# First modulation in two halves with the queries by feature tiles, and RWKV's first pair prepared among the products of k and v

## The reference, cut to what matters

```
def adaln_in(s, cvec, norm_g, mod_w, mod_b):
    m = jax.nn.silu(cvec) @ mod_w + mod_b
    shift, scale, gate = jnp.split(m, 3, axis=-1)
    return rmsnorm(s, norm_g) * (1.0 + scale) + shift, gate
...
    hx, gate_x = adaln_in(x, c_lat, norm_g, mod_w, mod_b)
    hc, gate_c = adaln_in(ctx, c_cx, norm_g, mod_w, mod_b)
    px = hx @ w_in
    pc = hc @ w_in
```

```
    r, k, v = products of lerp(0), lerp(2), lerp(3) with three 1024 x 1024 matrices
    w_log = -softplus(-(w0[d] + tanh(lerp(1) @ w1[d]) @ w2[d])) - 0.5 ;  decay = exp(-exp(w_log))
    a = sigmoid(a0[d] + (lerp(4) @ a1[d]) @ a2[d]) ;  k_d = k * (1.0 + (a - 1.0) * k_a)
    g = sigmoid(lerp(5) @ g1) @ g2 ;  kk = normalised k * k_k
```

## Time and profile before

| | |
|---|---|
| median of 3 runs | 4120.06 us (4116.69 to 4125.03) |
| the profiled execution's own time | 4123.75 us |
| its span in the profile | 4122.5 us (1.25 us lie outside) |
| TensorE busy | 90% of the span, 31840 instructions |
| VectorE, ACT, POOL busy | 40%, 29%, 33% |
| mean granted clock of TensorE | 0.936 |
| data moved | 263.76 MB, mean 64 GB/s |

### The profile page before, as it was taken

How to read it: one execution, slowest core, us unless ns; L and a number is a source line. 1 busy time by engine, 2 the same in 40 slices (tenths; PEclk the granted TensorE clock), 3 DMA queues, 4 the chain that set the end, 5 groups by cost and what they waited for, 6 DMA issues and landing times.

```text
span 4122.5 us, 72507 instructions
## 1 busy us (share of the span) xinstructions
PE 3700.5 (90%) x31840; PEld 2364.9 (57%) x31840; DVE 1657.6 (40%) x2926; ACT 1191.1 (29%) x2160; POOL 1377.5 (33%) x1214
## 2 busy tenths in 40 slices
PE   7998778999898988889899999898788888889998
PEld 3755565434444455555455555354566666748887
DVE  1344343223444122444433233532655555533334
ACT  3253222221212174432300000201555565520001
POOL 1320442011212112656432323351543343425444
PEclk9998687988999999989999999999899999989999
DMA  5420000521101211540111111222000000022222
GB/s 194 146 94 21 2 1 11 205 84 33 33 23 51 82 46 64 178 158 21 51 56 57 62 61 52 97 81 77 3 16 15 28 15 15 14 82 82 92 82 72
DMA packets 196131, 263.76 MB, mean 64 GB/s; under 512 B 6087, under 2 KB 151495, under 8 KB 193640
## 3 DMA queue, kind: packets, MB, share of 16 engines
q1 hardware_dynamic: 188880, 242.78, 17.6%
q10 hardware_dynamic: 6936, 16.35, 1.0%
HBM read 246.52 MB, written 12.58 MB: 63 GB/s over the span
## 4 chain that ended last, share of the span: by engine, by line
PE 72%; ACT 8%; DVE 6%; issue 6%; POOL 5%; DMA 2%; SPq 0%; ACTq 0%; DVEq 0%; POOLq 0%
PE ps L236 57%; PE ps L2943 2%; PE ps L759 2%; PE ps L484 1%; ACT mem L836 1%; PE ps L1959 1%; PE ps L786 1%; POOL mem L2846 1%; PE ps L774 1%; PE ps L378 1%; DMA mem<-rkv 1%; DVE mem L1159 1%; PE ps L493 1%; PE ps L1277 1%; DVE mem L817 1%
## 5 line engine op out<-in xcount | busy, mean ns | idle before, releaser
L236 PE MATMUL ps<-mem 64*64 64x64 f32 (+6 forms) x25344 | 2744.1, 304 | 203.2 <-ACT mem L661 35.9
L236 PEld LDWEIGHTS ps<-mem 64*64 64x64 f32 (+1 forms) x25344 | 1779.6, 156 | 1179.5 <-issue 606.0
L2846 POOL TENSOR_TENSOR mem<-mem 128x256 f32<-128x256 f32 (+1 forms) x264 | 238.5, 920 | 356.7 <-ACT mem L3301 185.3
L854 POOL TENSOR_SCALAR mem<-mem 128x768 f32<-128x768 f32 (+2 forms) x128 | 219.2, 1725 | 199.4 <-DVE mem L820 199.3
L2141 ACT ACTIVATE mem<-ps 128x384 f32<-128x384 f32 (+1 forms) x80 | 35.7, 446 | 838.8 <-PE ps L236 788.3
L2128 POOL TENSOR_TENSOR mem<-mem 128x512 f32<-128x512 f32 (+1 forms) x80 | 100.1, 1251 | 440.9 <-PE ps L236 392.2
L2152 DVE TENSOR_TENSOR mem<-mem,ps 128x384 f32<-128x384 f32 (+1 forms) x80 | 39.9, 499 | 442.9 <-PE ps L236 442.9
L2943 PE MATMUL ps<-mem 128*128 128x128 f32 x960 | 180.5, 307 | 32.3 <-DVE mem L2868 21.4
L591 POOL TENSOR_TENSOR mem<-mem 128x512 f32<-128x512 f32 (+1 forms) x72 | 74.7, 1062 | 393.3 <-ACT mem L586 391.6
L2876 ACT ACTIVATE mem<-ps 128x256 f32<-128x256 f32 (+1 forms) x220 | 101.5, 461 | 198.7 <-PE ps L2943 198.5
L2868 DVE TENSOR_TENSOR mem<-mem,ps 128x256 f32<-128x256 f32 (+1 forms) x220 | 109.5, 513 | 116.7 <-PE ps L236 116.1
(11 more groups left out here) (326 smaller groups left out, 4049.1 us busy)
## 6 DMA issues: line engine op xcount, KB each, us to landing
mem<-i_mod_w SPq DMA_DIRECT2D x48, 1024.0 KB, 6.8
mem<-i_ffn_wg SPq DMA_DIRECT2D x22, 1024.0 KB, 5.1
mem<-i_ffn_wu SPq DMA_DIRECT2D x22, 1024.0 KB, 5.2
mem<-i_e_w_in SPq DMA_DIRECT2D x16, 1024.0 KB, 6.0
mem<-i_o_w_in SPq DMA_DIRECT2D x16, 1024.0 KB, 5.6
mem<-i_ffn_wd SPq DMA_DIRECT2D x16, 1024.0 KB, 5.3
mem<-i_e_mod_w SPq DMA_DIRECT2D x12, 1024.0 KB, 6.0
mem<-i_o_mod_w SPq DMA_DIRECT2D x12, 1024.0 KB, 7.3
```

The source lines that it names most:

```text
L236: ins = e.h.matmul(out, l, r, start=(i == 0), stop=(i == n - 1))
L854: K.pool.h.tensor_scalar(w, w, stat(i, o, 1), None, MUL).then_inc(*nm.up(tag, i, o))
L2846: K.pool.h.tensor_tensor(m3(self.slot(l)), self.lraw, bm(C(K, f"cm{self.d}", l, 64), 2 * self.np), MUL).then_inc(*self.mk.up(key, l))
```

## The change

Two places are changed. At the start of the program:

- SP loads only the first 266 columns of the constants (`ident`, `ones`, `eps`, `sel`) at first; the others and ctx are loaded behind the second half of the modulation.
- The four jobs of the modulation become two halves: half 0 gives shift and scale of feature tiles 0 to 3 (jobs 0 and 8 of `e_mod_b`), half 1 those of tiles 4 to 7. They have a ring of four slots of their own. SP's order is half 0 (four slabs), two slabs of `e_w_in`, half 1 (four slabs), ctx, the other constants.
- x is normalised and modulated for tiles 0 to 3 after half 0, for tiles 4 to 7 after half 1 (`factors(j)` makes the scales of a half).
- The queries are done with `across=2`: four output tiles in four banks, feature tile by feature tile, and `beside` puts TensorE's steps of half 1 after feature tiles 1, 2 and 3, and the sums of ctx's squares after tile 5. ctx has a norm of its own (`nc`, "ec").

In RWKV:

- `jobs` is r, w, a, g, k, v.
- `Scan` is made before `rwkv_inputs`, with the first pair's tiles laid where `u` and `xx` lie (free once the last mixture is made). `Scan.ahead` advances front(0) on every engine by counted steps at the middle and end of the units of k and v (`AHEAD`), with banks from those that were just used (`FIRST`). `load_first` loads pair 0's r, k and head weights behind k's first unit, and its v behind v's first unit. v of pair 0 is turned in the middle of the last unit (`values_pe`, `values_act`).
- Before the scan only VectorE, ACT and POOL wait for the others' ends (`fence(but=K.pe)`); `run` begins with work(0).

The core of the diff:

```
+    mod = modulate(K, A, B)
+    ring = Ring(K, "mslab", [K.alloc(SLOT) for _ in range(4)], "e")
+    halves = [mod_stream(K, (4, 5), 6, mod_jobs(("e_mod_b", 4 * j, 4 * j + 4), ("e_mod_b", 8 + 4 * j, 12 + 4 * j)), ring) for j in range(2)]
...
+    def sp():
+        run(halves[0][2]())
+        linear_sp(K, I["e_w_in"], (0, 512))
+        run(halves[1][2]())
+        K.sp.h.dma_start(K.xc, I["ctx"]).then_inc(*lc.up(0, by=16))
+        K.sp.h.dma_start(K.cn[:, CN_FIRST:], I["consts"][:, CN_FIRST:]).then_inc(*lr.up(by=16))
...
+    def dve():
+        steps = halves[0][1]()
+        next(steps)
+        q = n.factors(K.dve, 0)
+        for j in range(2):
+            for k in range(4 * j, 4 * j + 4):
+                K.dve.h.tensor_tensor(tile(k), K.xt[:, k, :], q, MUL).then_inc(*ml.up("e", 0, k))
+            if j == 0:
+                for _ in steps:
+                    pass
+                factors(0)
+        run(halves[1][1]())
+        factors(1)
+
+    def act():
+        for j in range(2):
+            K.act.wait_ge(*sc.at("e", j, 1))
+            for k in range(4 * j, 4 * j + 4):
+                K.act.wait_ge(*ml.at("e", 0, k))
+                mod(k, 0, tile(k)).then_inc(*out.up("e", 0, k))
+
+    def beside():
+        steps = halves[1][0]()
+        yield
+        for _ in range(3):
+            next(steps)
+            yield
+        yield
+        nc.sums()
+        yield
     n.squares()
-    for _ in range(3):
-        next(steps)
+    steps = halves[0][0]()
+    next(steps)
     n.sums()
     run(steps)
...
+    nc.squares()
+    linear_pe(K, "nq", (0, 512), hap, RNG[:1], ALL, K.sig("qk_copy", "act"), beside(), across=2)
...
-    jobs = [("rr", 0, W[0], 1024, RNG[:1], 0), ("rk", 2, W[1], 1024, RNG, 512), ("rv", 3, W[2], 1024, RNG, 1280),
-            ("rw", 1, I["w1"], 128, RNG, (hw, ACT.Tanh)), ("ra", 4, I["a1"], 128, RNG, (ha, ACT.Copy)), ("rg", 5, I["g1"], 128, RNG[:1], (hg, ACT.Sigmoid))]
+    jobs = [("rr", 0, W[0], 1024, RNG[:1], 0), ("rw", 1, I["w1"], 128, RNG, (hw, ACT.Tanh)), ("ra", 4, I["a1"], 128, RNG, (ha, ACT.Copy)),
+            ("rg", 5, I["g1"], 128, RNG[:1], (hg, ACT.Sigmoid)), ("rk", 2, W[1], 1024, RNG, 512), ("rv", 3, W[2], 1024, RNG, 1280)]
...
-                for i, p in order:
+                for q, (i, p) in enumerate(order):
                     if p == 1:
                         units[n][i].take()
                     units[n][i].product(p)
+                    if i and p == (3 if i == 1 else 2):
+                        scan.ahead("pe", 4 * (n - 4) + i, "mid", [(q - j) % 8 for j in range(1, 5)])
...
+AHEAD = {(1, "mid"): 3, (2, "mid"): 8, (3, "mid"): 13, (5, "mid"): 16, (5, "end"): 19, (6, "mid"): 22, (6, "end"): 25}
+FIRST = {2: "ss", 3: "a", 5: "w0", 6: "w1", 7: "v"}
...
+    def ahead(self, e, unit, part, banks=None):
+        if banks and unit in FIRST:
+            self.first[FIRST[unit]] = banks
+        while self.steps[e] < AHEAD.get((unit, part), 0):
+            next(self.early[e], None)
+            self.steps[e] += 1
+        if (unit, part) == (7, "mid") and e in ("pe", "act"):
+            (self.values_pe if e == "pe" else self.values_act)(0)
...
+    def load_first(self, v):
+        K, b, s = self.K, self.bufs[0], self.ld[0]
+        if v:
+            K.sp.wait_ge(*s.at(0, "k"))
+            K.sp.h.dma_start(b[:, 1664:2432], K.rkv[0][:, 1280:2048]).then_inc(*s.up(0, by=16))
+            return
+        K.sp.h.dma_start(b[:, 0:384], K.ins["hpw"][0]).then_inc(*s.up(0, 0, by=16))
+        K.sp.h.dma_start(b[:, 384:1664], K.rkv[0][:, 0:1280]).then_inc(*s.up(0, "k", by=16))
...
-            run(f(0))
```

More of the change, by code:

```diff
@@ L383, in linear_pe @@
                         K.spent(held[j // 2][0], lin, tag, j)
+            if beside:
+                next(beside, None)
         i = 2 * across
@@ new lines, in even @@
+    sc, ml, out = K.sig("scales", "dve"), K.sig("nrm_mul", "dve"), K.sig("nrm_out", "act")
+    sq, acc, rs = [mem[:, 0:768], mem[:, 768:1536]], mem[:, 1536:2304], mem[:, 2304:3072]
+    n = Norm(K, "e", xt_ap(K), RNG[:1], lambda ri, k: (lx, (0,)), sq, acc, rs, (7,))
+    nc = Norm(K, "ec", xt_ap(K), RNG[1:], lambda ri, k: (lc, (0,)), sq, acc, rs, (7,))
+    halves = [mod_stream(K, (4, 5), 6, mod_jobs(("e_mod_b", 4 * j, 4 * j + 4), ("e_mod_b", 8 + 4 * j, 12 + 4 * j)), ring) for j in range(2)]
+    tile = lambda k: ht[:, k, 0:NX]
@@ L1023, in deltanet @@
 def deltanet(K, ht, hap, ot):
-    I, W = K.ins, K.ins["e_w_in"]
+    for e in (K.pe, K.dve, K.act, K.pool):
+        e.wait_ge(*K.sig("ld_rest").at())
     qT, kT = K.a3(4, NX), K.a3(4, NT)
@@ L2597, in rwkv @@
     mark1 = K.top
[L2598 to L2601, removed]
+    scan = Scan(K, hw, ha, hg, id64)
+    top, K.top = K.top, mark1
+    rwkv_inputs(K, hw, ha, hg, norm, scan)
+    K.fence(but=K.pe)
+    K.top = top
+    scan.run()
     yo_done = K.sig("fi_out", "dve")
@@ L2604, in rwkv @@
     yo = K.yo
-    K.ring.lend([(yo_done, (6,))], [(yo_done, (7,))], [(yo_done, (7,))])
+    K.ring.lend([(scan.wp, (7, d, 1, "wkv")) for d in range(2)], [(yo_done, (7,))], [(yo_done, (7,))])
     def ready(k, r0, rn):
@@ L2663, in operand @@
         return half(n, 2 * j, 1) if p == 7 else {5: t1, 6: t2, 4: t4}[p][:, j, :]
-    units = {n: [Seven(K, jobs[n][0], i, 4, 384, mem, lambda p, j, n=n: operand(n, p, j), wide[i % 2], b) for i, b in enumerate(seven_banks(order, 4))] for n in (1, 2)}
+    units = {n: [Seven(K, jobs[n][0], i, 4, 384, mem, lambda p, j, n=n: operand(n, p, j), wide[i % 2], b) for i, b in enumerate(banks)] for n in (4, 5)}
     def over(n):
@@ L2706, in dve @@
                 lerp(n, k)
-            if n - 1 in units:
-                results(n - 1)
+        for n in units:
+            results(n)
     def results(n):
@@ L2789, in sp @@
     def sp(t):
-        for tag, j, w, cols, rngs, _ in jobs:
+        for n, (tag, j, w, cols, rngs, _) in enumerate(jobs):
             linear_sp(K, w, (0, cols))
+            if n in units:
+                for x in range(2):
+                    K.sp.wait_ge(*st[x].at(8 + 16 * (n - 4) + x))
+                if n == 4:
+                    K.sp.wait_ge(*lp.at(3, KT - 1))
+                scan.load_first(n == 5)
         for i in range(t - 4, t):
@@ L3010, in loads @@
         K.settle(K.sp)
-        for hp in range(8):
+        for hp in range(1, 8):
             if hp >= 2:
@@ L3081, in front_act @@
             yield
[L3082 to L3087 removed]
+        if hp:
+            self.values_act(hp)
         A.wait_ge(*fd.at(hp, "max", 1))
```

165 lines of the change are left out of this document (100 added, 65 removed).

## The result

The changed kernel takes 4074.32 us (median of 4 runs, 4072.09 to 4082.58) beside 4121.92 for the kernel before (4 runs in turn with them, 4116.69 to 4125.03). The ratio is 0.9888, with a 95% interval of 0.9875 to 0.9901: faster by 1.1%, 47.6 us of medians. Forecast were 4077, in 4064 to 4092.

The account below looks back on a forecast made before the run. TensorE was taken as the bound (72% of the chain ending last), paying where it idles or runs at lower clock. RWKV −42 and start −3 gave −45: 4079 from the profiled execution, 4075 from the median, so 4077, range 4064 to 4092.

Parts of the forecast that it names:

- 1, v's last product to the inverse: RWKV, front(0) off the path: 49.8 us become 6.0 (4.5 to 8), gain 43.8 (41.8 to 45.3).
- 2, the front's work on TensorE in the units: RWKV, front(0)'s TensorE work among the unit products is not hidden: cost 7 us (5 to 13).
- 3, waits on the other engines: RWKV units: the front's steps on other engines are ready before TensorE asks, 0 us (bound 12); rival of stalls 0.12.
- 4, v's start: RWKV, v's first nine unit products run with next to no idle time, 23.3 us for 31.4: gain 8.1 (6 to 8.1).
- 5, k's start: RWKV, k's mixture and POOL's turns slow each other, 2.3 us idle: cost 2.5 us (0 to 6).
- the start: Start of the program: queries end at 72.1 us against 75.1, gain 3 (−7 to +1); rival of no gain 0.12.
- The thirteenth turn: k's start: POOL's last turn needed by product 5, there at 22.6 us, wanted at 24.0, so in time.
- The limit: RWKV units: TensorE comes to a bank held by VectorE's wait at `kk0` only past 38 us of k.
- The strict form of the rule: k's start: each turn waits for one mixture, thirteenth turn at 26.1 us, step 5 costing 4.4 instead of 2.5.
- the wait before tile 4: Start: TensorE waits some 1.9 us for bias, scales and ACT; a clock drop costing 1.7 only in the bound.
- the slow first products: Start: the query products' half-clock beginning costs 3 us, as before the change.
- ctx's sums: Start: 0.9 us on TensorE, plus 1 for ACT, which can square ctx only behind its last modulation.

Follow-up runs that it names:

- before_b: The kernel before, unaltered, profiled once more: 4120.98 us, one run.
- before_a: The kernel before, unaltered, profiled once more: 4117.38 us, one run.
- rwkv_only: The kernel before with only RWKV's part of the change: 4085.68 us, ratio 0.993.
- front_after: The changed kernel with pair 0's front run whole behind the inputs again, early load and new job order kept: 4102.06 us, ratio 0.9958.
- front_twice: The changed kernel with pair 0's sums and a computed twice and w four times on TensorE, same output: 4084.25 us, ratio 0.9916.
- late_load: The changed kernel with twelve more loads of the head weights before pair 0's on SP, delaying `kk0`: 4090.33 us, ratio 0.9934.
- after_again: The changed kernel once more, unaltered: 4072.6 us, ratio 0.99.
- start_better: The changed kernel with half 1's steps one feature tile earlier and half 0's rows and scales before the norm's products on VectorE: 4066.73 us, ratio 0.9871.

## Why the prediction was right, step by step

With more profiles the pair before and after can be set right. Four profiles with the old RWKV part have 299.2, 295.7, 298.6 and 295.7 (mean 297.3), five with the new one 254.3, 254.4, 256.0, 254.8 and 254.4 (mean 254.8). The gain is **42.5 us, forecast 42.4**. In the first pair it was 44.9. There k's products ran partly at the lower clock in the kernel before (65.20 us for the 196 records behind the first idle time of 2.42), as in `before_b` (65.06) and not in `before_a` (63.51), and so did r's last slab (38.94 for 104 records, 37.24 in `before_a`).

| step | forecast | measured |
|---|---|---|
| 1, v's last product to the inverse | 6.0 of 49.8 left, gain 43.8 | 6.1 left, gain 43.7 |
| 2, the front's work on TensorE in the units | +7 (5 to 13) | +6.4 |
| 3, waits on the other engines | 0 (to 12) | 0 |
| 4, v's start | −8.1 | −8.2: nine products in 23.2, no idle time |
| 5, k's start | +2.5 (0 to 6) | +1.8 |
| the start | −3 (−7 to +1) | −2.4 in the pair, −1.3 over eleven profiles |

That the total meets the forecast to 0.1 us is luck. The measured steps sum to −43.7, 1.3 more than forecast, nearly all in steps 2 and 5; about half of what is missing is something that no step has, the clock. In four of five profiles of the new part the 112 records of r's last slab, w, a and g came partly at the lower clock (43.20 us, with 0.65 granted from 2652.8 to 2657.0 after, and 41.51 in `rwkv_only`), and two of the four old ones, both at 295.7, have no such loss anywhere. With its 1.7 us taken off the new part's 254.3 would be 252.6, a gain of 43.1. The rest I did not trace.

*Step 1* is shown by `front_after`: with the front back behind the inputs the idle times of before are back one by one. *Step 2*: by the distance from each insertion to the next product they cost 1.30 (sums), 1.49 (a), 1.49 and 1.48 (w) and 0.65 (turns); the forecast had 1.45, 1.8, 2.9 and 1.2. `front_twice` shows that each is paid. a gives 1536 columns in the 1.49 in which w gives 768: its products alternate between the two halves of the array's rows. The Trainium skill says of such products that they run at the same time (TensorE: Matmul & The Clock Gate, Part 3), and the trace agrees.

*Step 3* is the one on which the forecast might have failed, and `late_load` shows why it did not: `kk0` came at

```profile
2730.40 0.62 DVE L3270 TENSOR_SCALAR mem<-mem 128x768 f32<-128x768 f32 x1 [7.09 <-DMA mem<-rkv]
```

that is 34.3 us after k's first product at 2696.05, forecast 35. VectorE waits 7.09 us there and TensorE not at all. The limit, forecast at 38, lies a little further out: of 28.9 us of lateness TensorE paid 22.1 by standing, so 6.8 were free, and `kk0` may come at 41. This is one measurement. *Step 5* had the right cause and a size too large. The thirteenth turn ended 22.9 us after k's mixtures began (forecast 22.6), with turns of 1.71 us as in the earlier trace rows:

```profile
2690.32 1.71 POOL L2807 TENSOR_TENSOR mem<-mem 128x384 f32<-128x384 f32 x1 [1.26 <-DVE mem L2749]
...
2710.39 1.71 POOL L2807 TENSOR_TENSOR mem<-mem 128x384 f32<-128x384 f32 x1
```

but k's first products took the mixtures nearly as fast as they came, with idle times of 0.73, 0.62 and less, not 2.3 in one piece. The strict form of the rule of the Trainium skill (SBUF — State Buffer, Who interferes with whom) would have had that turn at 26.1; the trace has it 3 us sooner, so here VectorE and POOL slow each other but do not exclude each other for their whole length.

*The start* came out near the sum with the single terms off to both sides. The first query product came at 31.93 (forecast 32), the last query ended at 71.9 (forecast 72.1). But the wait before tile 4 (1.59, forecast 1.9) did bring the clock down, 0.81 in the stretch from 55.2, which cost 1.8 us and was only in my bound. On the other side the slow first products cost 2.1 (9.12 us for 16) and not 3, and ctx's sums cost 0.9 without the 1 of waiting for ACT that I had added. Of the 3.3 us by which the queries end earlier 0.6 went to a wait that the sum does not have: the first key product now waits for ACT to copy a query tile out (0.59 before 72.45). In `after_again` the same wait of 1.59 did not bring the clock down (16 records in 7.13), and the next wait, on ctx's sums, was 0.84; of six profiles with this start three show the fall and three do not. `start_better` shows that the wait and the fall were there to be removed.

*What stays open.* The medians differ by 47.6 us; RWKV's 42.5 and the start's 1.3 are 43.8, and the other 3.8 are inside what the middle moves by from one execution to the next. (The first pair of spans differs by 51.7: 2.4 at the start, 4.6 in the middle, 44.9 in RWKV's part, −0.2 behind it.) Not explained is that six of eight runs of the new RWKV part with the old start took 4084.4 to 4092.5 us, where the kernel after took 4065.3 to 4082.6 in eight: the start's 1.3 us, or 2.4, do not make that difference. A middle of 2544.1 accounts for the one of the six that was profiled. The means of eight are 9.4 us apart (4083.5 and 4074.1), about the difference of the middles with the two starts; with the old RWKV part the start moves whole times by 1.8 only. A start that shortens the middle stays a possible cause, and more profiles of both would have to decide it.

## What to carry to other kernels

A chain that hops over four engines costs its whole length where nothing else runs, and only its TensorE time where it is cut into steps among products that TensorE has anyway: 49.8 us became 6.1 + 6.4. Price the inserted products in full, and find out how late the chain's first operand may come before what is queued behind its first wait holds the banks; here that was some 7 us of room, and beyond it each microsecond cost one and the clock something more. Work pulled forward at a start is worth what TensorE no longer waits for in all: 12.7 us of earlier first product were 1.3 to 2.4 us at the first key copy.

## What the runs showed of the hardware

The same code took different times, with TensorE's clock. Busy time of the middle in `rwkv_only`, then in `late_load` (columns as above):

```profile
78.60:2622.60 2544.00, 2321.12 (x10952) 1340.47 (x10950) 910.10 (x1634) 650.06 (x1161) 760.61 (x638) 0.92 0.20 66
```

```profile
79.60:2594.20 2514.60, 2286.29 (x10952) 1325.27 (x10951) 910.61 (x1634) 650.40 (x1161) 759.44 (x638) 0.93 0.20 67
```

The same 10952 records keep TensorE busy for 2321.12 and 2286.29 us, while VectorE, ACT and POOL differ by less than 1.2. The rows show the clock, 0.92 and 0.93, and not what made it differ. Over thirteen profiles this stretch took 2514.6 to 2544.1 us, a spread of 29.5 us, 0.7% of the whole; two profiles with the same start differ by up to 13 of them with the new one (2514.6 and 2527.9) and by up to 17 with the old one (2526.8 and 2544.1). For what a change does inside the stretches that it touches, the stretches are the finer measure. They say nothing of what it may do to the code between them, and for that whole times, or many profiles, are needed.
